# A hybrid attention and pooling decoder block on eight cores: one normalisation for two attention blocks, a new order of the projections, held first loads, and banks of its own for the output projection

## The reference, cut to what matters

```python
z = x @ w_in                                  # q, k, v (512 each) | pool input u (512) | gates (2048)
q, k = rope(q), rope(k)                       # 8 heads of 64
y_attn = moba_attention(q, k, v)              # own block of 256 causally, plus top 3 of the past blocks by q . mean(k_block)
y_pool = per group g (window w = 2, 4, 8, 16): (trailing mean over w - token) @ w_pool[g] * pool_scale
mix = (sigmoid(gate_a) * (y_attn @ w_branch_attn) + sigmoid(gate_p) * (y_pool @ w_branch_pool)) @ w_out
x = layer_norm(ALPHA * x + mix)
a, u = x @ w_ffn_gate, x @ w_ffn_up           # 2816 wide; a goes through a causal convolution of width 3
x = layer_norm(ALPHA * x + (gelu(conv(a)) * u) @ w_ffn_down)
```

## Time and profile before

| what | value |
|---|---|
| median of 3 runs | 1047.12 us (1046.24 to 1194.91) |
| profiled execution, its own time | 1046.32 us |
| its span, slowest core | 1044.8 us |
| spans of the 8 cores | 1035.3 to 1044.8 us |
| PE, DVE, ACT, POOL busy | 952.7, 627.4, 437.7, 264.8 us |
| mean granted TensorE clock, slowest core | 0.972 |

### The profile page before, as it was taken

The page is one execution under the profiler, slowest core; times in us unless marked ns, Lnnn a source line. Parts: engine busy times, 40 slices in busy tenths (PEclk is TensorE's granted clock), DMA queues, the critical chain, the costliest instruction groups (busy, mean ns, idle before and its releaser), DMA issues.

```text
span 1044.8 us, 17414 instructions; the slowest of 8 cores (1035.3 to 1044.8 us)
## 1 busy us (share of the span) xinstructions
PE 952.7 (91%) x4984; PEld 477.4 (46%) x4984; DVE 627.4 (60%) x1215; ACT 437.7 (42%) x760; POOL 264.8 (25%) x301
## 2 busy tenths in 40 slices
PE   3786887996999999999999898899999999999996
PEld 1243444653666665444444344444444444444443
DVE  5648887762443433265647778866566766665666
ACT  0133454664666665234343554554100555454000
POOL 3744343235123223345522233212000000000000
PEclk9889998996999999999999999999999999999999
DMA  9970011023223325966145654599431644441221
GB/s 147 169 121 24 31 29 34 23 53 54 38 54 50 63 31 98 180 157 160 57 117 116 134 143 82 111 223 164 98 112 61 162 81 71 74 80 22 81 102 60
DMA packets 42174, 95.77 MB, mean 92 GB/s; under 512 B 6560, under 2 KB 15264, under 8 KB 41440
## 3 DMA queue, kind: packets, MB, share of 16 engines
q0 software_dynamic: 22144, 52.37, 30.6%
q1 hardware_dynamic: 19936, 42.29, 12.3%
HBM read 125.89 MB, written 16.78 MB: 137 GB/s over the span
## 4 chain that ended last, share of the span: by engine, by line
PE 74%; DVE 13%; issue 5%; DMA 4%; ACT 1%; POOL 1%; DVEq 0%; ACTq 0%; POOLq 0%
PE ps L417 74%; DMA wout<-wout 2%; DVE t L437 2%; DMA xT<-xT 2%; DVE PLt L450 1%; DVE cbuf L450 1%; DVE hT L437 1%; DVE row L450 1%; DVE PT L761 1%; DVE nt L460 1%; DVE nb L752 1%; DVE km L571 1%; PE ps L421 1%; ACT cbuf L434 1%; POOL P L437 0%
## 5 line engine op out<-in xcount | busy, mean ns | idle before, releaser
L417 PE MATMUL ps<-x1T,wgu 128*128 128x512 bf16 x1408 | 313.9, 381 | 5.4 <-DVE row L450 3.8
L417 PEld LDWEIGHTS ps<-x1T,wgu 128*128 128x128 bf16 x1408 | 137.8, 98 | 174.4 <-issue 12.6
L450 DVE SCALAR_TENSOR_TENSOR cbuf<-abuf,small,cbuf 128x512 f32<-128x512 f32 x176 | 147.2, 837 | 107.7 <-ACT cbuf L434 97.4
L434 ACT ACTIVATE PT<-ps 128x512 bf16<-128x512 f32 (+1 forms) x288 | 155.6, 573 | 128.2 <-PE ps L417 121.6
L417 PE MATMUL ps<-wd,hT 128*128 128x512 bf16 x704 | 152.3, 379 | 0.0
L417 PE MATMUL ps<-PT,Vp 128*128 128x256 bf16 x576 | 108.5, 270 | 23.8 <-DVE PT L761 14.1
L417 PE MATMUL ps<-q,k 72*128 72x256 bf16 x576 | 109.4, 271 | 0.4 <-ACT PT L434 0.4
L417 PEld LDWEIGHTS ps<-wd,hT 128*128 128x128 bf16 x704 | 68.8, 98 | 83.2 <-issue 0.3
L434 ACT ACTIVATE abuf<-ps 128x512 f32<-128x512 f32 x88 | 52.4, 596 | 126.3 <-PE ps L417 122.5
L408 POOL DMA_DIRECT2D wgu<-wgu x44 | 24.0, 544 | 286.0 <-PE ps L417 283.9
L417 PE MATMUL ps<-xT,wqk 128*128 128x512 bf16 x256 | 71.4, 415 | 16.8 <-DMA xT<-xT 16.8
(11 more groups left out here) (96 smaller groups left out, 1063.6 us busy)
## 6 DMA issues: line engine op xcount, KB each, us to landing
wgu<-wgu POOLq DMA_DIRECT2D x44, 512.0 KB, 5.4
xres<-x SPq DMA_DIRECT2D x16, 512.0 KB, 3.8
x1s<-row SPq DMA_DIRECT2D x16, 512.0 KB, 3.0
row<-x1s SPq DMA_DIRECT2D x16, 512.0 KB, 11.6
out<-row SPq DMA_DIRECT2D x32, 256.0 KB, 2.0
wd<-wd POOLq DMA_DIRECT2D x22, 256.0 KB, 7.6
wga<-wg POOLq DMA_DIRECT2D x16, 256.0 KB, 4.9
wgp<-wg POOLq DMA_DIRECT2D x16, 256.0 KB, 5.9
```

What stands on the lines that cost most here:

```text
L417: S.op("pe", lambda e: e.matmul(out, lhsT, rhs, start=start, stop=stop), reads=[lhsT, rhs], writes=[out])
L434: S.op("act", lambda e: e.activation(out=out, in_=in_, func=func, **kw), reads=rd, writes=[out])
L450: S.op(eng, lambda e: e.scalar_tensor_tensor(out=out, in0=in0, scalar=scalar, in1=in1, op0=op0, op1=op1), reads=rd, writes=[out])
```

## The change

- The first x chunk comes in four loads. SP's loads of the rope tables and `small` wait for its second quarter, POOL's load of wu 0 (and all behind it) for its third quarter, `AM` for wv.
- `norm` works on both query blocks of a head at once (512 columns), and the accumulator bank holds both.
- `kmeans` takes four accumulating Copies on ACT in place of a DVE reduction. Group 0 of the pooling is one POOL subtraction, and its DVE operation goes.
- `proj` is written out: in chunks 2 and 3 keys, pooling inputs and values first, the queries last. `pool_sub` and `pool_mm` are put off by 1 and 2 tile ends. The block choice of chunk 3 runs inside `merge(0)`.
- The item prices are 7.0, 3.4, 2.1, 2.1.
- `oproj` has banks 0 to 2 to itself, the others share 3 to 7 until O1 is over. `o_tr` copies on ACT alone. O1's factor is 3.0.

```diff
+    stt_ = T("lnst", [128, 8, 12], F32, o)
+    junk = T("junk", [128, 256], BF16, o); o += 512
...
+    rs = T("rs", [128, 16], F32, o); o += 64
+    ps0 = T("psc0", [128, 1], F32, o); o += 32
...
-    nt = [T(f"nt{i}", [128, 256], F32, PT0 + (6 + i) * KB) for i in range(2)]
-    nb = [T(f"nb{i}", [128, 256], F32, PT0 + (8 + i) * KB) for i in range(2)]
+    nt = T("nt", [128, 512], F32, PT0 + 6 * KB)
+    nb = T("nb", [128, 512], F32, PT0 + 8 * KB)
...
-    wba = [T(f"wba{i}", [128, 4, 128], BF16, o_ * KB) for i, o_ in enumerate((172, 174, 170))]
-    wbp = [T(f"wbp{i}", [128, 4, 128], BF16, o_ * KB) for i, o_ in enumerate((173, 175, 171))]
-    sga = [T(f"sga{i}", [128, 512], F32, (176 + 2 * i) * KB) for i in range(2)]
-    sgp = [T(f"sgp{i}", [128, 512], F32, (180 + 2 * i) * KB) for i in range(2)]
-    m1 = [T(f"m1_{i}", [128, 512], F32, (184 + 2 * i) * KB) for i in range(2)]
-    m2 = [T(f"m2_{i}", [128, 512], F32, (188 + 2 * i) * KB) for i in range(2)]
+    wba = [T(f"wba{i}", [128, 4, 128], BF16, o_ * KB) for i, o_ in enumerate((168, 170, 178))]
+    wbp = [T(f"wbp{i}", [128, 4, 128], BF16, o_ * KB) for i, o_ in enumerate((169, 171, 179))]
+    sga = [T(f"sga{i}", [128, 512], F32, o_ * KB) for i, o_ in enumerate((172, 174))]
+    sgp = [T(f"sgp{i}", [128, 512], F32, o_ * KB) for i, o_ in enumerate((176, 182))]
+    m1 = [T(f"m1_{i}", [128, 512], F32, o_ * KB) for i, o_ in enumerate((184, 186))]
+    m2 = [T(f"m2_{i}", [128, 512], F32, o_ * KB) for i, o_ in enumerate((188, 190))]
...
+    def ld_cast(dst, src, after=()):
...
+    def ld(dst, src, after=()):
...
     ld_cast(wqk[0][:], wqk_d[0])
-    ld_cast(xc[0][:, 0:4, :], xT_d[0][:, 0:4, :])
-    ld_cast(xc[0][:, 4:8, :], xT_d[0][:, 4:8, :])
+    for i in range(4):
+        ld_cast(xc[0][:, 2 * i:2 * i + 2, :], xT_d[0][:, 2 * i:2 * i + 2, :])
     ld_cast(wqk[1][:], wqk_d[1])
-    rope_load(0)
-    ld(small[:], small_d)
-    ld(AM[:], am_d)
+    first = [xc[0][:, 2:4, :]]
+    rope_load(0, first)
+    ld(small[:], small_d, first)
     for i in range(4):
-        ld_cast(wu[:, i, :, :], wu_d[i])
+        ld_cast(wu[:, i, :, :], wu_d[i], [xc[0][:, 4:6, :]] if i == 0 else ())
         if i < 3:
...
     ts("dve", hb[:], bgate, 0.5, None, ALU.mult)
+    ts("dve", ps0[:], pscale[:, 0:1], 0.5, None, ALU.mult)
+
+    ld(AM[:], am_d, [wv[:]])
...
-        while post and post[0][0] <= 0:
-            post.pop(0)[1]()
-
-    def rope_pair(c, w, st):
-        tq = tqs[c // 3]
+        due = [e for e in post if e[0] <= 0]
+        post[:] = [e for e in post if e[0] > 0]
+        for e in due:
+            e[1]()
...
+        yield from rope_pair(c, 4 * g + 2 * kind, st, tqs[1 if c == 3 and kind == 1 else 0])
...
-        S.op("dve", lambda e: e.tensor_reduce(out=km[:], in_=kst[:].rearrange("p a (n t) -> p (a n) t", t=256),
-                                              axis=AX.X, op=ALU.add), reads=[kst[:]], writes=[km[:]])
+        for i in range(4):
+            src = kst[:, i // 2, (i % 2) * 256:(i % 2) * 256 + 256]
+            S.op("act", (lambda i, src: lambda e: e.activation(out=junk[:], in_=src, func=AF.Copy, accum_out=km[:, i:i + 1]))(i, src),
+                 reads=[src], writes=[junk[:], km[:, i:i + 1]])
...
+        if g == 0:
+            tt("pool", PLt[0][:], cur[:, 15:527], cur[:, 16:528], ALU.subtract)
+            return
...
+        if g == 0:
+            return
...
-        act(PL[c // 2][:, g, (c % 2) * 512:(c % 2) * 512 + 512], bk[:, :], AF.Copy, scale=pscale[:, g:g + 1])
+        act(PL[c // 2][:, g, (c % 2) * 512:(c % 2) * 512 + 512], bk[:, :], AF.Copy,
+            scale=ps0[:, 0:1] if g == 0 else pscale[:, g:g + 1])
...
-        act(U_[:, 0:16], uh[:, g, :], AF.Copy)
         act(U_[:, 16:528], bk[:, :], AF.Copy)
+        if c == 0 and g == 0:
+            act(U_[:, 15:16], U_[:, 16:17], AF.Copy)
+        else:
+            act(U_[:, 0:16], uh[:, g, :], AF.Copy)
         act(uh[:, g, :], U_[:, 512:528], AF.Copy)
```

`proj` anew (the old body goes; it is printed above):

```diff
+        def K(g):
+            return kq_pair(c, g, 0)
+
+        def Q(g):
+            return kq_pair(c, g, 1)
+
+        def V(r):
+            return v_tile(c, r)
+
+        def U(g):
+            yield from u_tile(c, g)
+            defer(1, (lambda c, g: lambda: pool_sub(c, g))(c, g))
+            defer(2, (lambda c, g: lambda: pool_mm(c, g))(c, g))
+
+        def rows(c):
+            gate_rows(c)
+            done.add(("R", c))
+
+        c = 0
+        yield from K(0)
+        yield from U(0)
+        yield from Q(0)
+        yield from U(1)
+        next(late)
+        yield from K(1)
+        yield from U(2)
+        next(late)
+        yield from Q(1)
+        yield from U(3)
+        next(late)
+        rope_load(1)
+        for r in range(4):
+            yield from V(r)
+        done.add(("R", 0))
...
+        c = 1
...
+        next(late, None)
+        yield from Q(0)
+        yield from U(1)
+        yield from K(1)
+        yield from U(2)
+        yield from Q(1)
+        yield from U(3)
+        rope_load(2)
+        for r in range(4):
+            yield from V(r)
...
+        c = 2
+        yield from K(0)
+        yield from U(0)
+        yield from V(0)
+        yield from U(1)
+        yield from V(1)
+        yield from K(1)
+        yield from U(2)
+        yield from V(2)
+        yield from U(3)
+        yield from V(3)
+        while ("A", 0) not in done:
+            yield None
+        yield from Q(0)
+        yield from Q(1)
+        rope_load(3)
+        c = 3
+        yield from U(0)
+        yield from V(0)
+        gate_scores(2)
+        yield 4
+        yield from K(0)
+        yield from U(1)
+        yield from V(1)
+        yield from K(1)
+        rows(2)
+        yield 2
+        yield from U(2)
+        yield from V(2)
+        yield from U(3)
+        yield from V(3)
+        mg_load()
+        mg_load()
         while ("A", 1) not in done:
             yield None
+        yield from Q(0)
+        yield from Q(1)
+        defer(2, lambda: (gate_scores(3), mg_load()))
+        defer(7, lambda: rows(3))
         yield from merge(0)
 
```

```diff
-            acc = ACC[acc_of[i] % 2]
+            acc = ACC[h % 2]
+            o = (b % 2) * 256
             pt = PT[i % 5]
-            last = i + 1 == len(items) or items[i + 1][2:4] == (items[i + 1][2], items[i + 1][2])
-            if p == b:
-                mm(acc[:, 0:256], vl(h, 2 * p), pt[:, 0:256], True, False)
-                mm(acc[:, 128:256], vl(h, 2 * p + 1), pt[:, 256:384], False, last)
+            last = i + 1 == len(items) or items[i + 1][2] != b
+            if b == 0:
+                mm(acc[:, 0:128], vl(h, 0), pt[:, 0:128], True, True)
+                mm(acc[:, 128:256], vl(h, 0), pt[:, 128:256], True, False)
+                mm(acc[:, 128:256], vl(h, 1), pt[:, 256:384], False, True)
+            elif p == b:
+                mm(acc[:, o:o + 256], vl(h, 2 * p), pt[:, 0:256], True, False)
+                mm(acc[:, o + 128:o + 256], vl(h, 2 * p + 1), pt[:, 256:384], False, last)
             else:
-                mm(acc[:, 0:256], vl(h, 2 * p), pt[:, 0:256], False, False)
-                mm(acc[:, 0:256], vl(h, 2 * p + 1), pt[:, 256:512], False, last)
-            return last
+                mm(acc[:, o:o + 256], vl(h, 2 * p), pt[:, 0:256], False, False)
+                mm(acc[:, o:o + 256], vl(h, 2 * p + 1), pt[:, 256:512], False, last)
+            return last and b % 2 == 1
...
-            s = acc_of[i] % 2
+            acc = ACC[h % 2]
             lo, oo = (64, 0) if h % 2 == 0 else (0, 64)
             osl = slice(oo, oo + 64)
-            n_, m_ = nt[s][osl, :], nb[s][osl, :]
-            r_ = rs[osl, 0:8]
-            dtr(n_, acc[lo:lo + 64, 0:256])
+            n_, m_, r_ = nt[osl, :], nb[osl, :], rs[osl, :]
+            dtr(n_, acc[lo:lo + 64, :])
             recip(r_, n_.rearrange("p (j r) -> p j r", r=32)[:, :, 0])
-            rb = bass.AP(r_.tensor, r_.offset, [list(r_.ap[0]), [1, 8], [0, 32]])
+            rb = bass.AP(r_.tensor, r_.offset, [list(r_.ap[0]), [1, 16], [0, 32]])
             mr = m_.rearrange("p (j r) -> p j r", r=32)
             S.op("dve", lambda e: e.transpose(mr, rb), reads=[r_], writes=[m_])
-            bl = b % 4
-            tt("dve", ATT[b // 4][osl, h // 2, bl * 256:(bl + 1) * 256], acc[osl, 0:256], m_, ALU.mult)
+            cl = (c % 2) * 512
+            tt("dve", ATT[c // 2][osl, h // 2, cl:cl + 512], acc[osl, :], m_, ALU.mult)
...
-            while ("V", c) not in done:
+            while ("R", c) not in done:
...
+                tile_end()
...
+                tile_end()
...
+    OB = [ps[0], ps[1], ps[2]]
+    ob_rr = [0]
...
+            bk = obank()
...
+        pT = obank()[:, :].bitcast(BF16)
...
-        if T_ % 2 == 0:
-            act(dst, src, AF.Copy)
-        else:
-            cp("dve", dst, src)
+        act(dst, src, AF.Copy)
...
-    A0 = Stream(attn([0, 1, 2, 3], {0: 5.0, 1: 2.6, 2: 2.6, 3: 2.6}))
+    A0 = Stream(attn([0, 1, 2, 3], {0: 7.0, 1: 3.4, 2: 2.1, 3: 2.1}))
...
```

(78 more changed lines are left out.)

12 lines of the change are left out of this document (4 added, 8 removed).

## The result

The changed kernel takes 1054.1 us (1052.6 to 1056.1, 4 runs) against 1046.2 us (1045.4 to 1047.1, 3 runs) for the one before; ratio 1.0076, 95% interval 1.0052 to 1.0100. The forecast was 1016 us and faster. The change is slower by 8 us, and that little is the sum of large parts of both signs. Five marks, taken from the slowest core of each profiled execution, show it: the end of chunk 0's projection, the issue of wout's load (which follows attention's last item), the first matmul of the FFN, the first of the down-projection `p8(0)`, and the end.

The account below looks back on a forecast made before the run. It took PE to be held by DVE's in-order queue in the projection stage before merge(0), where half the loss lay. Stage 1 -37.7, stage 2 banks -2, late weights +9 gave -30.7 us from 1047.1: 1016 us, range 998 to 1040.

Parts of the forecast that it names:

- Start and chunk 0: First loads and chunk 0: held loads bring 3 us, pooling waits 1.4; chunk 0 ends at 61 instead of 65.4 us.
- Stage 2, banks: Output projection beside merge(1) and FFN: transposes' copies leave DVE, three own banks; 2 us gained, bounds -5 and +6.
- Late weights: Start of the down-projection: five wd loads issued after it begins, PE waits for them; +9 us, bounds 3 and 11.
- spreading O1 over more steps: Second output projection beside the FFN: O1 spread by factor 3.0, part of the 2 us gain taken for stage 2.
- kmeans on ACT: Projection chunks: DVE gets 1.2 us back, 8 times; ACT's 10 to 19 us over eight lie beside other work.
- Stage 1: Projections, attention and merge(0): 367.6 us against 405.3, 37.7 us less.
- The factor from DVE's share: Chunks 1 to 3: DVE's busy share sets time over PE's ideal; 1.14, 1.15, 1.08, so 40, 47 and 51 us.
- The norm: Attention's normalisation on DVE: 2.3 us for 512 columns, 0.7 us less per head and chunk; operations not lengthened by GpSimd.
- Rival 1: Chunks 1 to 3: chains, not DVE, hold PE; factors stay near 1.3, 156 us instead of 138, total 1034; chance 0.2.
- Rival 2: Whole kernel: DVE's relief is complete, factors 1.05, and late weights cost 3 us; total 1001; chance 0.15.
- Rival 4: Stage 1: transposes of 512 columns cost double and the order changes nothing; some 15 us gain remain, total 1039; chance 0.11.
- Rival 3: Beside merge(0): ACT becomes the bound, 193 items take 218 us, 52 more; total 1068; chance 0.04.

Follow-up runs that it names:

- run 1: Changed kernel with AM's load emitted after chunk 0's rope reload, without its wait for wv: 1037.5 us, ratio 0.9917 to the kernel before.
- run 5: Run 4's kernel with the output projections and their transposes back on the common rotation over all eight banks: 1014.7 us, ratio 0.9702.
- the second of runs 13 to 15: Run 10's kernel with three own banks for the output projection beside the FFN only: 1020.3 us (+9.8).
- run 3: Changed kernel with O1's price factor back at 2.6 from 3.0: 1041.7 us, ratio 0.9953 to the kernel before.
- run 9: Run 4's kernel with kmeans back on DVE, one reduction in place of the four Copies on ACT: 1022.0 us, ratio 0.9770.
- run 10: Changed kernel with AM's load free of its wait, O1's factor 2.6, common banks and kmeans on DVE: 1010.5 us, ratio 0.9653 to the kernel before.
- run 4: Changed kernel with both edits, AM's load without the wait and O1's factor at 2.6: 1025.1 us, ratio 0.9798 to the kernel before.

## Why the prediction was wrong

- **The order of SP's queue: the step that failed.** The prediction's "Start and chunk 0" counted the bytes of SP's held loads. It never looked at what stands behind the load of AM, and had this part 4.4 us better than before (61 us). The trace of before had what was needed: wv's landing at 42 us and the key moves from 26 us on. Measured, chunk 0 ends 11.3 us later (76.7), and the wait costs 16.5 us in all (run 1). With AM free chunk 0 ends at 63.2 us, 2.2 us better than before.
- **Banks.** The step "Stage 2, banks" named the mechanism, bounded it at 6 us and then took a gain of 2 without a reason for that choice. Measured: 10.5 us of cost (run 5), 9.8 beside the FFN alone (the second of runs 13 to 15). PE's waits for the row operation rise from 6.4 to 11.7 us, and on some cores matmuls at the low clock follow them (see the last section).
- **Late weights.** The mechanism was right: f = 18, five loads, PE standing at wd 17 and after. The term was 9 us (bounds 3 and 11) and measured 12.4 (run 3), outside its bounds: from p8(0) to the end the slowest core loses 9.9 us, most others about 12. PE's waits for wd are 6.6 us on the slowest core and up to 9.7 on the others, and after the longest of them single matmuls take 0.58 us in place of 0.38, as at the low clock. Part of the miss is in the sum itself: it stops at wd 20. Carried on to wd 21, the last load, its own steps give a landing at 13.3 us, reached at 4.5, so 8.8 us of wait and 10.5 in all. The 2 us that I credited to spreading O1 over more steps did not exist (run 3).
- **kmeans on ACT** was put at nothing, covered by ACT's idle time. It costs 3.1 us net (run 9). The cover was there, the order was not: ACT and DVE both work in order, and DVE waits for the last of the Copies.
- **Stage 1** was forecast at -37.7 us. With AM free it is -25.7 us to wout's issue, with kmeans put back as well -34.2 (run 10; the medians of the eight cores say -27.4 and -31.9). Over PE's ideal time chunks 1 to 3 cost 1.21, 1.13 and 1.26 in run 4, where 1.14, 1.15 and 1.08 were forecast. The factor from DVE's share failed most in chunk 3, where that share was low but the block choice sits in one piece: the longest wait there ends with a long piece of DVE's work in a row.
- **The norm**: 2.3 us forecast, 2.36 measured (the reciprocal takes 248 ns, not 200). Its long operations, with one SBUF input at most, take 714, 705 and 689 ns, as the slope of the operations with a PSUM operand says; they are not lengthened. The Trainium skill (SBUF — State Buffer, "SBUF: two separate sides") lets a DVE operation contend with GpSimd only if it runs in a 2-port mode or has two SBUF inputs; the trace agrees.
- **The sum.** Measured minus forecast is 38 us. The AM wait gives 16.5 of them, the banks 12.5 (10.5 and the 2 credited), the late weights 3.4 beyond their 9, kmeans 3.1. Some 3 us are left, about what stage 1 lacks in run 10. (The prediction's 905 us for all matmuls should be 903, 4240 units at 0.213 us; nothing hangs on it.)
- **The rivals.** Rival 1 (chains hold PE, factors near 1.3) is neither shown nor gone: chunks 1 to 3 take 147.8 us in run 4 and 144.8 in run 10, between the forecast's 138 and the rival's 156. Rival 2 fell with the late weights, 12.4 us and not 3. Rival 4 fell with the transposes, which cost 1.6 times and not double. Rival 3 (ACT bound beside merge(0)) fell: PE is unbroken there from 264.9 us on. Its row, with columns as in the earlier trace rows, has ACT at 73%.

```profile
264.90:397.70 132.80, 132.37 (x929) 87.64 (x930) 50.43 (x92) 97.55 (x182) 30.67 (x41) 1.00 0.27 45
```

The forecast of 1016 us is nearly what the change gives without three of its errors (1014.7, run 5), but that is luck, by other sums: it had the late weights' 9 us in it, and stage 1 too good.

## What to carry to other kernels

A wait put on a load holds everything behind it on the issuing engine's queue. List what that queue must issue before the awaited thing lands, and what buffers those free; put the load where nothing urgent follows. Fixing shares of a rotating resource (here banks) took slack from one side or the other in both splits tried; it is worth a test by itself. Look at all cores before you explain 3 us of the slowest one. When a stream is slowed by a price, compute which loads depend on its end, and whether they still land in time.

## What was not expected of the hardware

- An accumulating activation comes with a second instruction, ACTIVATION_READ_ACCUMULATOR, of 189 ns.
- A norm of twice the columns costs 1.6 times on each long operation (447 to 714, 440 to 705, 422 to 689 ns), so each carries 0.16 to 0.18 us that does not depend on its size (an estimate, by a straight line through the two sizes).
- A wait of PE can cost more than it lasts. Chunk 0 of the changed kernel ran at a mean granted clock of 0.78, that of the kernel before at 0.86:

```profile
15.00:76.70 61.70, 35.64 (x127) 13.75 (x127) 14.34 (x31) 13.33 (x36) 32.73 (x43) 0.78 0.77 130
```

- The same wait is not followed by the low clock on every core. In the run with own banks beside the FFN, all eight cores have 11.7 us of row waits, but core 3 takes 209.4 us from FFN to p8(0) at a clock of 0.96, core 1 203.5 at 0.99. After the same wait of 3.42 us, four matmuls take 1.87 us on core 3 and 1.02 on core 1 (first row core 3). Against run 10 most cores lose 5 to 6 us in this stretch, about what their waits grew, and the slowest 10.5; the kernel's time follows the slowest. Why one core falls to the low level and another does not is open.

```profile
577.10 1.87 PE L419 MATMUL ps<-wout,mix 128*128 128x512 bf16 x4 [3.42 <-DVE row L452]
575.08 1.02 PE L419 MATMUL ps<-wout,mix 128*128 128x512 bf16 x4 [3.42 <-DVE row L452]
```
